# A reordered dense part, and a router fed by halves, in a two-layer decoder kernel

## The reference, cut to what matters

```
h = h + concat(o_nsa, o_conv, o_hgrn) @ w_out
h = h + cross_attention(rmsnorm(h), rmsnorm(mem), wq, wkv, wo)
xf = rmsnorm(h);  lg = xf @ w_rg + b_rg;  le = xf @ w_re + b_re      # the router: 4 + 32 columns
grp = argmax(lg); top2 = top_k(softmax(le of grp), 2); gate = p_grp * top_p / sum(top_p)
h = h + sum over the two experts of gate * (silu(xf Wg) * (xf Wu)) Wd
```

## Time and profile before

| | |
|---|---|
| median of 3 runs | 1397.89 us (1397.1 to 1401.44) |
| profiled execution, its own time | 1394.63 us |
| its span in the trace | 1392.6 us |
| PE busy | 1230.2 us (88%) |
| DVE, ACT, POOL busy | 491.2, 246.1, 77.0 us |
| DMA | 455.28 MB, mean 327 GB/s |

### The profile page before, as it was taken

How to read it: one execution, slowest core, us unless ns; L and a number is a source line. 1 busy time by engine, 2 the same in 40 slices (tenths; PEclk the granted TensorE clock), 3 DMA queues, 4 the chain that set the end, 5 groups by cost and what they waited for, 6 DMA issues and landing times.

```text
span 1392.6 us, 26052 instructions
## 1 busy us (share of the span) xinstructions
PE 1230.2 (88%) x10688; PEld 731.3 (53%) x10688; DVE 491.2 (35%) x1094; ACT 246.1 (18%) x569; POOL 77.0 (6%) x104
## 2 busy tenths in 40 slices
PE   7989997998898898898899898979989988898986
PEld 6867655544343354344488776654434443453433
DVE  4266525432232233222243544353223222322323
ACT  3013214111111111111110222231111111111111
POOL 0221300010000000000031112000000000000000
PEclk9999998999999999999999999979999999999999
DMA  8331339699999999999944013588999999999994
GB/s 353 120 128 62 121 120 422 252 427 429 428 428 429 429 429 428 428 428 429 415 169 156 31 61 121 237 367 345 429 428 428 429 428 429 428 427 429 428 429 172
DMA packets 33268, 455.28 MB, mean 327 GB/s; under 512 B 3776, under 2 KB 4160, under 8 KB 5312
## 3 DMA queue, kind: packets, MB, share of 16 engines
q1 hardware_dynamic: 33216, 454.59, 77.9%
HBM read 453.53 MB, written 1.05 MB: 326 GB/s over the span
## 4 chain that ended last, share of the span: by engine, by line
PE 56%; DMA 34%; DVE 5%; issue 2%; ACT 2%; SPq 1%; DVEq 0%; ACTq 0%
PE bank L514 54%; DMA share<-in_w_dn 17%; DMA share<-in_w_gu 14%; DMA streams<-in_w_gu 3%; PE bank L573 1%; SPq L390 1%; DVE small L1570 1%; DVE rest L1863 1%; PE bank L744 1%; DVE share L1550 1%; DMA share<-in_mem 0%; ACT streams L1115 0%; ACT ring L1184 0%; PE bank L1027 0%; DVE h L1486 0%
## 5 line engine op out<-in xcount | busy, mean ns | idle before, releaser
L514 PE MATMUL bank<-share,rest 128*32 128x512 f32 (+1 forms) x2432 | 280.3, 533 | 31.6 <-DMA share<-in_w_dn 31.6
L514 PE MATMUL bank<-dense,rest 128*32 128x256 f32 (+2 forms) x1824 | 188.2, 479 | 13.3 <-DMA share<-in_w_gu 10.4
L514 PE MATMUL bank<-ring,rest 128*32 128x256 f32 (+1 forms) x1792 | 175.9, 479 | 16.9 <-DMA share<-in_w_gu 15.1
L514 PEld LDWEIGHTS bank<-share,rest 128*32 128x32 f32 x2432 | 92.3, 114 | 135.4 <-issue 94.7
L514 PE MATMUL bank<-streams,dense 128*128 128x256 f32 (+2 forms) x928 | 153.4, 340 | 6.9 <-ACT streams L1115 4.6
L514 PE MATMUL bank<-rest 96*128 96x512 f32 (+1 forms) x288 | 122.0, 579 | 34.4 <-DVE rest L1863 34.4
L514 PEld LDWEIGHTS bank<-streams,dense 128*128 128x128 f32 (+1 forms) x928 | 132.9, 177 | 23.7 <-issue 6.2
L514 PE MATMUL bank<-rest,xhat 128*128 128x96 f32 x1088 | 142.5, 286 | 2.6 <-DVE rest L1772 2.6
L514 PEld LDWEIGHTS bank<-rest,xhat 128*128 128x128 f32 x1088 | 131.7, 198 | 18.0 <-issue 15.9
L514 PEld LDWEIGHTS bank<-dense,rest 128*32 128x32 f32 (+1 forms) x1824 | 70.6, 112 | 132.0 <-issue 99.7
L514 PEld LDWEIGHTS bank<-ring,rest 128*32 128x32 f32 x1792 | 66.5, 111 | 128.7 <-issue 96.3
(11 more groups left out here) (233 smaller groups left out, 989.6 us busy)
## 6 DMA issues: line engine op xcount, KB each, us to landing
share<-in_w_dn SPq DMA_DIRECT2D x64, 2048.0 KB, 19.8
ring<-in_w_gu SPq DMA_DIRECT2D x48, 2048.0 KB, 21.4
dense<-in_w_gu SPq DMA_DIRECT2D x48, 2048.0 KB, 24.7
share<-in_w_gu SPq DMA_DIRECT2D x24, 2048.0 KB, 22.9
dense<-in_w_units SPq DMA_DIRECT2D x18, 2048.0 KB, 9.5
streams<-in_w_gu SPq DMA_DIRECT2D x8, 2048.0 KB, 27.9
dense<-in_w_units SPq DMA_DIRECT2D x4, 1024.0 KB, 5.9
dense<-in_w_units SPq DMA_DIRECT2D x2, 1184.0 KB, 5.6
```

The lines of the kernel that those rows point to most:

```text
L514: return pe.matmul(out_ap, lhsT=lhsT, rhs=rhs, start=start, stop=stop, skip_group_check=True)
```

## The change

Computed results stay what they were; instructions move, and the second tile's way to the router is cut in two.

PE and DVE, levels of the recurrence:

```diff
 PE    two_T("cb", ...)
-      half_level(8)
       wait("cmp_p") ... transposes cmp_t
+      half_level(8)
 ...
       values(0)
+      half_level(16)
       scores(2)
-      half_level(16)
       turn_probs(1); hg; values(1)
+      half_level(32)
       scores(3)
-      half_level(32)
       turn_probs(2); ch; values(2)
+      half_level(64)
       scores(4)
-      half_level(64)
       turn_probs(3)
 DVE   rotate("rk", krot_b, "k", True)
-      level_mask("lv4", 3); level_q(16)
       ... cmp_s: maxima, differences ...
       done("cmp_shifted", 27)
+      level_mask("lv4", 3); level_q(16)
       maxima(0)
 ...
       normalise(1)
+      level_mask("lv16", 5)
       maxima(2)
-      level_mask("lv16", 5)
 ...   (lv32 and maxima(3), lv64 and maxima(4) in the same way)
```

PE, the recurrence's product:

```diff
       turn_probs(4)
+      values(4)
       settled("off_0", "hi"); ... av ...
-      values(4)
       turn_probs(5)
```

Cross part:

```diff
 PE    cross_query(0)
+      turn("y", "cross", 1)
       bank_done(memory_values(1), "memv")
       settled("cq0")
       scores(NN)
-      turn("y", "cross", 1)
       cross_query(1)
 ACT   turned("y", G_CROSS, 1) now ahead of the two copies of memv, before behind them
 DVE   turned("y", G_CROSS, 1) now ahead of maxima(NN), before behind it
```

Router, second tile:

```diff
 PE
+     def turn_half(j):
+         settled(f"co{2 + j}")
+         bk = bank_free(pe, l, f"zT{2 + j}")
+         for d in range(4):
+             k = 4 * j + d
+             ins = pe.transpose(bk[:, d * P:(d + 1) * P], h[:, 1, k * P:(k + 1) * P], ident)
+         bank_done(ins, f"zT{2 + j}")
-     def route(tt):
-         settled(f"zT{2 * tt}", f"zT{2 * tt + 1}")
-         for k in range(8):
+     def route(tt, j):
+         settled(f"zT{2 * tt + j}")
+         for k in range(4 * j, 4 * j + 4):
              ins = mm(bk[:, tt * 36:(tt + 1) * 36], xnT[:, k, tt * P:(tt + 1) * P], ...)
-     route(0)
-     turn("z", "ffn", 1, h)
-     bank_done(route(1), "rt")
+     turn_half(0)
+     route(0, 0)
+     turn_half(1)
+     route(0, 1)
+     route(1, 0)
+     bank_done(route(1, 1), "rt")
 ACT
-     norm("ffn", 1)
+     for n in range(2):
+         wait_drained(act, l, f"co{2 + n}")
+         alone(act)
+         ins = act.activation(xhat[:, 1, n * 512:(n + 1) * 512], h[:, 1, n * 512:(n + 1) * 512], ACT.Square,
+                              accum_out=half_ssq[:, n:n + 1])
+     ins.then_inc(ev("squares1_ffn"), 1)
 DVE
-     norm("ffn", 1)
+     wait("squares1_ffn")
+     link(V.tensor_tensor(ssq[:, 1:2], half_ssq[:, 0:1], half_ssq[:, 1:2], ADD))
+     own("rstd1_ffn", inverse_root(link, rs[:, 1:2], ssq[:, 1:2], 1.0 / D))
```

More of the change, by code:

```diff
@@ L57 @@
 PLACE = {name: (b, n) for b, names in USES.items() for n, name in enumerate(names)}
-DVE_STEPS, POOL_STEPS = 144, 23
+DVE_STEPS, POOL_STEPS = 145, 23
 N_UNITS = 12
@@ L214, in hymba @@
         mem_rs, mem_ssq = small[:, 92:94], small[:, 94:96]
+        half_ssq = mem_ssq
         root_x, root_t = small[:, 172:180], small[:, 180:188]
@@ L1238, in _ @@
                 keep_queries(0)
+                turned("y", G_CROSS, 1)
                 bk = bank_full(act, l, "memv")
@@ L1242, in _ @@
                 bank_drained(ins, "memv")
-                turned("y", G_CROSS, 1)
                 exps(NN)
@@ L1634, in _ @@
                 rotate("rk", krot_b, "k", True)
-                level_mask("lv4", 3)
-                level_q(16)
                 cp = cmpP.rearrange("p (g c) -> p g c", c=NCMP)
@@ L1650, in _ @@
                 done("cmp_shifted", 27)
+                level_mask("lv4", 3)
+                level_q(16)
                 maxima(0)
@@ L1679, in _ @@
                 V.tensor_copy(mixT[:, 2:4, 0:P], two(banks[7][:, 0:512])[:, :, 0:P]).then_inc(ev("mix0_heads23"), 1)
+                level_mask("lv32", 6)
                 maxima(3)
-                level_mask("lv32", 6)
                 level_q(128)
@@ L1684, in _ @@
                 normalise(3)
+                level_mask("lv64", 7)
                 maxima(4)
-                level_mask("lv64", 7)
                 keep_pT(3)
```

## The result

The changed kernel took 1388.86 us (median of 4, 1387.41 to 1389.85) against 1398.05 (1397.1 to 1401.44) for the kernel before: ratio 0.9919, 95% interval 0.9903 to 0.9935. A second comparison, in the experiments, gave 1387.66 and 0.9920 (0.9895 to 0.9946). Faster, then, with 1391.5 forecast. Two runs far outside the rest, 1865.51 of the kernel before (beside e1 to e4) and 2534.91 of e2, count in no ratio.

What follows compares the result with a forecast made beforehand. Each layer's end was taken as its expert part's first loop load, waiting on PE, plus fixed DMA work. Terms: −8.4 without the clock, +2.0 for the clock, so −6.4: 1397.89 to 1391.5 us, range 1383.5 to 1399.

Steps and rivals of the forecast that it cites:

- lv4 behind the compressed scores: Ahead of group 0's scores in the dense part: wait shrinks from 3.61 to 1.3 us; gain 2.3 per layer.
- The clock there: Group 0's scores and cb: clock may stay up after the shorter gap; 1.5 per layer taken, bounds nothing or 2.2.
- half_level(8): Behind cmp_t, before group 0's turning: two transposes go into an existing wait; no gain, half a microsecond either way.
- half_level(16), (32): Ahead of hg and ch: gaps of 1.76 and 1.16 go, a new wait of 0.3 comes; gain 2.6 per layer.
- half_level(64): Ahead of scores(4): hi waits for ACT and follows 1.1 us later, behind a gap of about 2.8; a loss.
- values(4): Ahead of av: waits for ACT's copies, starts 1.4 us later; gap grows from 1.74 to 3.1; a loss.
- The clock at these two places: Low clock behind the gaps at hi and av: 1.25 per layer for hi, +1.5 over today for av.
- y1: Cross part, y1 turned before the second memory values: group 6's turning comes later; loss 0.8 per layer.
- Router: Router by halves: PE goes on without a gap; gain 2.3 and 2.9, with 0.5 per layer held back for the clock.
- The slower rival: Clock falls before hi and stays down to its end, 7.2 more per layer; +7.6 in all, 1405.5; chance 0.10.
- conditions under which I said I would be wrong: First load moves more than the end; hi or values(4) don't wait for ACT; scores and cb keep 2.08, 8.44.
- the clock that pays everything back: Rival: clock falls in the 1.3 gap, ahead of hi, at av and in the router; +1.6, about 1399; chance 0.14.

Runs made afterwards that it cites:

- e1: The kernel before with only the router by halves, dense part in its old order; 1395.37 us, ratio 0.9981 to the kernel before.
- e4: Changed kernel with av ahead of values(4), scores(4) ahead of half_level(64) and y1's turn behind the cross scores, as before; 1379.31 us, ratio 0.9856.
- e2: The kernel before with only the reordered dense part and y1's move, router as before; 1396.58 us, ratio 0.9981.
- e11: e8 with two useless products of 512 columns in the 1.27 us gap ahead of scores(0); 1376.29 us, ratio 0.9827.
- e7: Changed kernel with ScalarE's two off copies moved ahead of exps(4) and the copy of group 3; 1382.69 us, ratio 0.9882.
- e6: Changed kernel with useless products filling its two new gaps, ahead of hi and of values(4); 1382.28 us, ratio 0.9887.
- e5: The changed kernel again, unaltered, in a second comparison; 1387.66 us, ratio 0.9920 to the kernel before.
- e10: e2 with e8's two edits (off copies first, av ahead of values(4)), so without the router part; 1384.42 us, ratio 0.9892.
- e8: Changed kernel with the two off copies ahead of exps(4) and av ahead of values(4); 1369.46 us, ratio 0.9787, the fastest version.
- e9: e2 (no router part) with the useless products of e6 in the two gaps; 1388.42 us, ratio 0.9918.
- e3: Changed kernel with av put ahead of values(4) again, as in the kernel before; 1385.26 us, ratio 0.9907.
- e12: e11 with y1's turn put back behind the cross scores, as in the kernel before; 1375.92 us, ratio 0.9842.

## Why the prediction was right, step by step

The sum was −6.4; by the medians it was −9.2, with the sign and the mechanism (what starts the first load starts earlier) as said. The steps can be held only against the traced pair, where they come to −5.7:

- *lv4 behind the compressed scores*: right. Gap 1.27, and 2.3 gained in both layers.
- *The clock there*: wrong. Scores and cb kept 2.08 and 8.77 in layer 0, 1.16 and 8.40 in layer 1; in all the gain was 0.1, not 3.0. The short gap is enough: with it filled (e11) they take 1.16 and 7.12. I had leaned on the 1.76 ahead of hg, which cost layer 0 nothing, and had left out layer 1, where the same gap had cost hg 8.83 against 7.14 (kernel before, layer 1):

```profile
809.32 8.83 PE L514 MATMUL bank<-dense,streams 128*128 128x256 f32 x32 [1.76 <-DVE share L1550]
```

- *half_level(8)*: right. A gap of 0.97 has come ahead of group 0's turning and shorter ones have gone; from the end of cb to the start of cc it is 7.4 us in both kernels.
- *half_level(16), (32)*: right in their waits (hg and ch without a gap, 0.24 ahead of level 32), low in size. I took 2.6 per layer; scores(0) to ch gained 3.4 and 5.8. About 1.8 of layer 1 is hg's clock, back at 7.07. And a gain that I had not seen: with the level directly ahead of the scores the two run as one group of 24 products in 2.03. From that group to ch it is 3.07 (125.77 to 128.84); scores, mask products and level in the old order took 3.59 to the same place (130.84 to 135.59, less the gap of 1.16). That is 0.5 at each such place, of which the third, ahead of off, goes into hi's wait. No run takes this gain apart.
- *half_level(64)*: right, ch to hi +1.29 and +1.02 (forecast +1.1), though the gap itself is 3.42 for 2.8, since PE gets there sooner. It was ScalarE's order, as said; e7 shows that the price was not necessary.
- *values(4)*: its wait right (3.05 for 3.1).
- *The clock at these two places*: the term that was mis-sized. I counted 1.25 per layer for hi and, for av, 1.5 over today in both together. From hi to wo0 the layers lost 5.5 and 5.3. Of that the wait of values(4) is 1.3 (in e7, with hi at full clock, it starts 13.52 behind hi; av of before 12.21): the clock took about 4 per layer over today, where I had 2. With the gaps filled (e6) hi and av are back at full clock. It was hidden in the total by the first half's larger gain.
- *y1*: right, +0.71 and +0.72 for 0.8.
- *Router*: right, and larger: −2.65 and −3.27 for −2.3 and −2.9. The clock did not fall inside the new stretch (24 products in 2.77, as fast as the 16 in 1.87 before), so the 0.5 held back was not needed in this execution; in e1's layer 1 it did fall there (3.12).
- *First load earlier by 3 to 4 in each layer*: 2.18 and 4.89, of which the change's stretches hold 1.15 and 4.50. In layer 0 the loads issued ahead did not start earlier (197.69 for 197.47).
- *The slower rival*: its price of 6.3 per layer leaves out the 1.6 of av that stands in its own sum; with it, 5.5 would have been enough.

Of the conditions under which I said I would be wrong, one came true, scores and cb. The clock was mis-sized by 2.9 us there and by 4 at hi and av; the time came out because these errors stood against gains that I had sized too low, among them 1.8 of hg's clock and the 0.5 per place, which I had not seen. That they balance is luck; the waits and their places are not. The rival nearest to what happened in the dense part is the clock that pays everything back; it did so there (+1.25 and −0.94) and not in the router.

The Trainium skill ("TensorE: Matmul & The Clock Gate", Part 1) says that the point at which the clock changes in a run is not tied to the kernel's start and differs between runs of one kernel. The traces agree: av of layer 1 took 4.53 in one execution of the changed kernel and 2.89 in another (e5), with the same gap of 3.05 or 3.04 ahead of values(4).

What stays open is where the fall goes. Two parts that gain 2.7 each gain 10 together, putting av back gains 2 to 3 and moving the off copies 5 but both together 18, and e10 stands 15 over e8. The mean granted clocks of the runs differ in the same sense; that the clock is the cause of the whole is not shown. Nor does the length of a gap decide: 1.27 ahead of scores(0) cost the clock in 20 layers of 20; 1.62 ahead of hi, where e6 and e9 have useless products in front, in none of four; 1.74 ahead of av in 10 of 16, one of the two layers in the kernel before, e1, e3, e4, e8 and e10, both in e11 and e12. What decides, and whether a fall avoided in one place turns up in the next, no run here settles.

## What to carry to other kernels

Price a new gap of TensorE twice: as a wait, and as the low clock of the forms behind it, at the worse of the two durations that the trace shows for them in any layer. When an order moves work ahead of a wait, read the queue of the engine that ends the new wait: here two copies stood behind an exponential and copies that were needed only later, and moving them, with av put back, was worth 18 us, more than the change itself. And when two kernels are within a few microseconds, read where a stretch begins and ends in both traces before believing a difference of their totals.

## What was not expected of the hardware

A gap of 1.27 us was enough for TensorE's clock to fall from 2.4 to 1.2 GHz, in every layer traced with it, and useless products in a gap can pay: 5.4 us per run in e6, with no useful instruction released earlier by them. The same gap of 1.74 cost the clock in some layers and not in others of one execution (av 5.01 and 2.86 in e8). And in layer 1 of e1 the clock fell within the router's small products (3.12 for 2.77), with PE busy without a break for 9 us before.
